# Down weights of the routed experts issued from ScalarE's queue instead of SyncE's, in a two-block transformer kernel with a mixture of experts

## The reference

```
h = modulated, normalised x                                  # [512, 1024]
hid = silu(h[t] @ w_gate_2[l, e]) * (h[t] @ w_up_2[l, e])     # 1024 -> 256
y[t] += weight[t, e] * (hid @ w_down_2[l, e])                # 256 -> 1024
y[t] += shared expert of h[t]
```

## Time and profile before

| what | value |
|---|---|
| median of 3 runs | 4001.08 us (3995.71 to 4007.47) |
| the profiled execution's own time | 3992.74 us |
| its span | 3990.9 us |
| instructions | 48312 |
| TensorE (PE) busy | 3383.3 us, 85% |
| VectorE (DVE) busy | 1579.6 us, 40% |
| ScalarE (ACT) busy | 948.2 us, 24% |
| GpSimd (POOL) busy | 200.2 us, 5% |
| DMA, all queues | 748.63 MB, mean 188 GB/s |
| q1 (SyncE) | 628.83 MB, 41.9% of 16 engines |
| q10 (ScalarE) | 50.33 MB, 3.7% |
| q0 (GpSimd) | 67.51 MB, 4.3% |

### The profile page before, as it was taken

One profiled execution on the slowest core, in us unless ns is written; L12 is line 12 of the kernel. 1 busy time (PEld: TensorE's weight loads), 2 busy tenths in 40 slices (PEclk: granted clock), 3 DMA queues, 4 the chain that ended last, 5 costly groups with the idle time before them and its releaser, 6 DMA issues. The chain is left out here.

```text
span 3990.9 us, 48312 instructions
## 1 busy us (share of the span) xinstructions
PE 3383.3 (85%) x14925; PEld 2114.9 (53%) x14926; DVE 1579.6 (40%) x3974; ACT 948.2 (24%) x2004; POOL 200.2 (5%) x204
## 2 busy tenths in 40 slices
PE   4887869997999687997799999847899779999985
PEld 2744546665777546663444444434666544444443
DVE  2273535445656354234322222254533342222225
ACT  2263423113323243212011111113412211111111
POOL 0000000000000000000111111100000001111110
PEclk7888879998999888999899999978999879999998
DMA  3202022643454311301899999642121159999974
GB/s 119 96 1 70 6 71 77 190 146 110 149 178 151 108 32 43 85 22 53 330 408 400 406 393 407 276 199 68 43 62 44 53 209 418 398 409 383 394 303 190
DMA packets 287135, 748.63 MB, mean 188 GB/s; under 512 B 25883, under 2 KB 167581, under 8 KB 230788
## 3 DMA queue, kind: packets, MB, share of 16 engines
q1 hardware_dynamic: 233988, 628.83, 41.9%
q0 software_dynamic: 27648, 67.51, 4.3%
q10 hardware_dynamic: 25344, 50.33, 3.7%
HBM read 721.06 MB, written 58.72 MB: 195 GB/s over the span
## 5 line engine op out<-in xcount | busy, mean ns | idle before, releaser
L2302 PE MATMUL up_ps<-experts,x_turned 128*64 128x512 f32 (+1 forms) x2256 | 696.7, 622 | 26.3 <-DMA experts<-in_w_up_dram 25.7
L2302 PEld LDWEIGHTS up_ps<-experts,x_turned 128*64 128x64 f32 (+1 forms) x2256 | 262.1, 161 | 383.8 <-issue 383.3
L256 DVE TENSOR_TENSOR pieces_lo<-weights,pieces_hi 128x512 fp32r<-128x512 f32 (+1 forms) x412 | 272.4, 682 | 299.1 <-ACT pieces_hi L250 297.5
L250 ACT CAST pieces_hi<-weights 128x512 fp32r<-128x512 f32 (+1 forms) x412 | 244.4, 614 | 484.7 <-PE products L268 104.7
L2326 PE MATMUL y_ps<-experts,hid_turned 128*64 128x512 f32 (+1 forms) x1128 | 345.7, 601 | 1.6 <-ACT hid_turned L2383 1.6
L2461 DVE TENSOR_TENSOR hid_seats<-up_ps,gated 128x256 f32<-128x256 f32 x94 | 57.5, 612 | 609.6 <-ACT gated L2376 609.6
L266 PE MATMUL gate_ps<-h_hi,pieces_hi 128*128 128x512 f32 x624 | 262.6, 421 | 37.6 <-DVE pieces_lo L256 31.9
L266 PE MATMUL products<-h_hi,pieces_hi 128*128 128x512 f32 x464 | 188.9, 407 | 90.9 <-DVE pieces_lo L256 90.9
L268 PE MATMUL gate_ps<-h_hi,pieces_lo 128*128 128x512 f32 x624 | 247.6, 397 | 0.0
L267 PE MATMUL gate_ps<-h_lo,pieces_hi 128*128 128x512 f32 x624 | 247.3, 396 | 0.0
L2326 PEld LDWEIGHTS y_ps<-experts,hid_turned 128*64 128x64 f32 (+1 forms) x1128 | 117.6, 154 | 222.0 <-issue 222.0
(11 more groups left out here) (399 smaller groups left out, 5041.6 us busy)
## 6 DMA issues: line engine op xcount, KB each, us to landing
experts<-in_w_gate_dram SPq DMA_DIRECT2D x141, 1024.0 KB, 11.8
experts<-in_w_up_dram SPq DMA_DIRECT2D x141, 1024.0 KB, 17.2
experts<-in_w_down_dram SPq DMA_DIRECT2D x141, 1024.0 KB, 15.4
ada_weights<-in_w_ada_dram ACTq DMA_DIRECT2D x48, 1024.0 KB, 5.3
rows_sb<-results SPq DMA_DIRECT2D x16, 2048.0 KB, 24.1
weights<-in_w_in_dram SPq DMA_DIRECT2D x57, 512.0 KB, 5.5
weights<-in_w_in_dram SPq DMA_DIRECT2D x12, 2048.0 KB, 9.7
weights<-in_w_out_dram SPq DMA_DIRECT2D x6, 2048.0 KB, 8.7
```

Of the source, the lines that this page charges most:

```text
L250: act.copy(self.like(view, self.hi[:, i % self.BUFFERS, :, :]), view).then_inc(s["hi_ready"], 1)
L256: dve.tensor_tensor(lo, view, hi.bitcast(F32), ALU.subtract).then_inc(s["lo_ready"], 1)
L2302: made = pe.matmul(up_ps[part, b, :].rearrange("p (h n) -> p h n", h=2), xT[:, b, k, part], experts.up(b + i)[:, :, k, :], start=(k == 0), ...
```

## The change

`load_down` moves from SyncE's program to ScalarE's, with the same waits, slots and sources. SyncE keeps `load_up` alone. ScalarE issues `load_down(0,0)` and `load_down(0,1)` at the start of its program, before it reads `end`. In `both(r)` it issues `load_down(r,0)` ahead of `silu(r,0)`, and `load_down(r,1)` between `weigh(r-1,1)` and `copy(r,1)`. The number and size of the transfers stay the same.

```diff
--- before.py
+++ after.py
@@ -2195,27 +2195,14 @@
                     for i, e in enumerate(es):
                         experts.load_up(sp, b + i, e)
 
-                def load_down(r, b):
-                    es = experts_of(sp, r, b)
-                    if past(r, 1):
-                        all_waited(sp, down_made[b], 2 * r)
-                    for i, e in enumerate(es):
-                        experts.load_down(sp, b + i, e)
-
                 load_up(0, 0)
                 load_up(0, 1)
-                load_down(0, 0)
                 end = end_of(sp)
                 load_up(1, 0)
-                load_down(0, 1)
                 load_up(1, 1)
-                load_down(1, 0)
                 with sp.Fori(2, end + 1) as r:
                     load_up(r, 0)
-                    load_down(r - 1, 1)
                     load_up(r, 1)
-                    load_down(r, 0)
-                load_down(end, 1)
 
             @block.gpsimd
             def _(pool):
@@ -2361,6 +2348,13 @@
 
             @block.scalar
             def _(act):
+                def load_down(r, b):
+                    es = experts_of(act, r, b)
+                    if past(r, 1):
+                        all_waited(act, down_made[b], 2 * r)
+                    for i, e in enumerate(es):
+                        experts.load_down(act, b + i, e)
+
                 def copy(r, b):
                     j = 2 * r + b
                     act.wait_ge(s["turned"], j + 1)
@@ -2391,6 +2385,8 @@
                     act.activation(y[:, b, 512:1024], y_ps[:, 1, :], ACT.Copy,
                                    scale=note[:, bass.ds(j, 1), 2]).then_inc(s["y_act"], 1)
 
+                load_down(0, 0)
+                load_down(0, 1)
                 end = end_of(act)
                 copy(0, 0)
                 silu(0, 0)
@@ -2401,8 +2397,10 @@
                 copy(1, 0)
                 copy_hidden(0, 1)
                 def both(r):
+                    load_down(r, 0)
                     silu(r, 0)
                     weigh(r - 1, 1)
+                    load_down(r, 1)
                     copy(r, 1)
                     copy_hidden(r, 0)
                     silu(r, 1)
```

## The result

The changed kernel takes 4033.28 us (median of 5, 4024.27 to 4034.3) against 4001.08 us. The ratio is 1.007, with a 95% interval of 1.0051 to 1.0089: slower by 0.7%, 28 us by the ratio (32 by the medians). A second set of runs of the same kernel gave 1.007 again (1.0055 to 1.0085).

A forecast was written before the change was run, and what follows sets the result against it. DMA and TensorE were taken as level in the two expert passes. Terms of 0 + 5 + 8 = +13 us on the 4001.08 us median gave 4014 us; range 3978 to 4052, the forecast's own 4005 to 4035.

The forecast's parts named there:

- rival B: In the loop, the critical up transfer is late in all 45 periods: 4046 to 4082 us; chance 0.15.
- Rival A: Whole kernel: nothing measurable, within 0.3%, since bytes and slots are unchanged and DMA stays the bound; about 4003 us; chance 0.23.
- What bounds the kernel: In the two routed_experts passes DMA and TensorE are level; up(r,1) alone waits for weights, about 2.6 us per longer stall.
- Work taken off SyncE: Per period SyncE loses 3 of 9 transfers with their register loads and waits; worth 0 us.
- Work on ScalarE: load_down(r,1) ahead of copy(r,1) adds 1.8 us of queue work; 2 us, counted as covered; bounds 0 to 13.
- The second queue in the loop: Down weights served beside the up loads put 1.05 MB more ahead of the critical transfer; 5 us, ends 0 and 81.
- The start: At each pass's start, down loads in a second queue delay the first gather; 4 us per pass, 8 in all.
- Rival D: ScalarE's issue time shows: 0.6 us in 22 periods, +13 us, 4027 with the other terms; inside the range, no separate chance.
- the signs that I had named: In the passes: in_w_up_dram waits rise, gathers land in about 12 us, first transposes wait 9 to 10 us.
- Rival C: In the loop, two queues keep DMA fuller and TensorE sets the pace: 3953 us, half of it 3977; chance 0.17.
- The rule that issuing from several engines only saves the sequencer's time: Skill page's sentence on issuing engines; by it alone the result would be 4001 us, as issue time is hidden here.

The follow-up runs named there:

- e5: Changed kernel with load_down(r,1) behind copy(r,1) and copy_hidden(r,0), and iteration 0's down loads behind copy(0,0): 4005.26 us, ratio 1.0016.
- e8: Changed kernel with the two register loads of load_down(r,1) moved ahead of silu(r,0), its issues left before copy(r,1): 4006.48 us, ratio 1.0013.
- e10: Changed kernel with load_down(r,1) behind both copies and iteration 0's down loads behind copy(0,0), run once more: 4007.91 us, ratio 1.0012.
- e4: The changed kernel again, unaltered, for a second profile: 4029.14 us, ratio 1.007.
- e1: Changed kernel with load_down(r,1) moved behind copy(r,1) and copy_hidden(r,0), still in ScalarE's queue: 4012.57 us, ratio 1.0031.
- e2: Kernel before, all loads on SyncE, with four unused register loads on ScalarE between weigh(r-1,1) and copy(r,1): 4011.45 us, ratio 1.0027.
- e9: Changed kernel with load_down(r,1) behind copy(r,1) and copy_hidden(r,0), early loads of iteration 0 kept, run again: 4009.98 us, ratio 1.0014.
- e11: Kernel before with eight unused register loads on ScalarE between weigh(r-1,1) and copy(r,1): 4158.77 us, ratio 1.0408.
- e12: Kernel before with two unused register loads on ScalarE between weigh(r-1,1) and copy(r,1): 4001.21 us, ratio 0.9999.

## Why the prediction was right, and where its terms were off

The sign and the range were right: slower, 4033 us in 3978 to 4052, with 4014 forecast. The shift was +28 us by the ratio against +13. The sum was short in one term. That the range held is in part luck: its upper end, 4052, came from rival B, which didn't happen (`up(r,1)` waits for weights 10 times and not 45, and DMA's share stays at 0.98). The forecast's own range, 4005 to 4035, held with 2 us to spare. Rival A is excluded by the interval, which begins at 1.0051. The chances were also added up a little wrong: by their own shares no change had 0.40 and slower 0.45, not 0.37 and 0.48.

- *What bounds the kernel:* right. The critical wait was `up(r,1)`'s for its weights, and with the change undone in parts (e5, e8, e10) it stands there as before.
- *Work taken off SyncE, 0:* nothing speaks against it. e5 and e10 have it and are no faster, but no run has it without the second queue.
- *Work on ScalarE, 2 us and then counted as covered, bounds 0 to 13:* **this is the term that was mis-sized.** It measures 16 us (e4 less e1, on one chip) and 11 us without the queue (e2). The start was right: the work begins with `weigh`, as VectorE's 0.28 us had suggested. The amount was not, 2.60 us against 1.8. I had added only the medians of two kinds of instruction, 0.153 + 0.268 and 0.096 + 0.374, and left out the second address instruction, the check, the move of the address, the 0.03 us between any two instructions and the waits. A register load takes 0.63 us and an issue 0.56. With 2.60 in my own sum the copy ends at 3421.07 + 2.60 + 0.58 = 3424.25, and `up(r,1)` starts 0.6 to 0.7 us late; 0.69 is measured. That my upper bound of 0.6 us comes near it is luck, for it rested on a start behind `weigh` that no run shows. The count was short too: 35 of 45 periods, not 22. And then I put it down as covered. In the changed kernel DMA gives back about half: 24.2 us of waits for the copy are new, and those for weights are 11.6 us shorter.
- *The second queue in the loop, 5 us, bounds 0 to 81:* right as far as the runs can tell. e5 and e10 give 0.14%, 6 us, and e10's interval reaches 0. The mechanism is seen in the landing times (10.3 us for down weights, 10.8 for scatters). The page "DMA: Bandwidth & Descriptors" of the Trainium skill has this sharing between queues in its section "Queues, rings and completion order", and the trace agrees; the low end was the nearer one, since the critical wait didn't grow (22 and 23 times, 25.6 and 26.2 us, against 24 and 25.7).
- *The start, 8 us, bounds -10 to 8:* 4.7 us of waiting in the rows, 1 to 9 us in the times. The cause was right (with the loads issued later, the wait is back at 5.4 to 6.1 us), the size some 2.3 us per pass and not 4.
- *Rival D* (ScalarE's issue time) was the largest part of the result, and I had priced it at 13 us at most. Of the signs that I had named, the waits for `in_w_up_dram` went the other way (fewer and shorter, not more), the gathers landed in 10.8 us and not in 12, and the first transposes waited 8 us and not 9 to 10. *Rival C* found nothing: with the copy first, DMA moves 399 and 400 GB/s, as with one queue.
- *The rule that issuing from several engines only saves the sequencer's time* (the Trainium skill, page "DMA: Bandwidth & Descriptors", section "Issuing engines are not separate DMA queues") says nothing of what the issues cost the engine that takes them over. Here its sequencer's time was the price. SyncE had time to spare and ScalarE hadn't, at that place.

The parts add up: 16 (ScalarE's work) + 5 (start, by the rows) + 6 (the queue) = 27 us, against 28 measured. The first is a difference of two ratios and so uncertain by some 8 us; the third is not clear of zero. The sum is a weak test, for the 16 are what e1 leaves of the 28. What it tests is whether start and queue, 11 us, make the 12 that e1 stands above the kernel before; e9, the same kernel as e1 on another chip, stands only 6 above, and with it ScalarE's work would be 22 us.

No version beats the kernel before. The best form of the change, with the register loads early (e8) or the copy first and a late start (e5, e10), is level with it or 0.1 to 0.2% slower.

## What to carry to other kernels

Before a DMA issue moves to a compute engine, look at what stands behind it in that engine's order and how much cover it has: here 0.7 us of delay were free, 1.8 us cost 11, and 4.1 us cost 163. When you price queue work, take the distance from one start to the next in a trace and not the sum of the instructions' durations: that gave 0.42 us for a register load that took 0.63. Read addresses into registers in a place where the engine is idle anyway, and put the issue behind the instruction that others wait for. And in this loop, where DMA was busy for 0.98 of the time, a second queue added no bandwidth (399 and 400 GB/s with the copy first, 402 and 399 before), it only changed which transfers landed sooner.

## What the runs showed of the hardware

- ScalarE's queue ran ahead under the instruction of its engine. In all 45 periods of e2, of e11, of e12 and of the changed kernel the first register load of the plan began within 0.1 us of the start of the ACTIVATE ahead of it and 0.6 us before its end; in e8 the first DMA issue went out under it too (2328.00, with the end at 2328.41), in all 45 periods. What stands behind them on the engine waits for all of them: the copy came 0.05 us behind `weigh` with nothing between (the kernel before), 0.7 with two register loads, 1.8 with four, 4.1 with eight.
- A register load from SBUF took 0.63 us in the queue with its address arithmetic and check, of which the load itself is 0.28, and an issue with an address from a register 0.56 us, of which the issue itself is 0.34 (changed kernel).
- After each of the 45 gaps of 2.4 to 3.3 us on TensorE in e11, the next 32 matmuls took 8.7 to 9.2 us instead of 7.09; the granted clock over two such periods was 0.94 of the full 2.4 GHz. After gaps of 0.4 to 0.9 us in the changed kernel it was so in 11 of 35 cases (8.66 us at 2150.91, 7.09 at 2179.27).
- Down weights landed in 10.3 us from their own queue and in 15.2 from the common one, with the same bytes per period. In pass 1 of e4 all 144 transfers of SyncE's queue landed in their order of issue, and so did all 72 of ScalarE's; of the 215 pairs that were issued one behind the other in either queue, 25 landed the other way round.
